# Thirty-two pairs of projections of an fp32 transformer layer turned from eight half products each into seven

## The chip, the cores and the metric

One core of a Trainium2 chip runs the whole program in one launch. The metric is the device time of that core in microseconds, the median over the runs. Each comparison with the kernel before is made on the same chip.

## The reference, cut to what matters

The program computes two blocks in fp32. The second block normalises 512 tokens of 2048 features (`h`) and projects them by one wide matrix `w_in_2` into pooling, sliding-window attention (SWA), gated linear attention (GLA), memory attention and four merge gates:

```
p = h @ w_in                      # h: 512 x 2048
pool_v, pool_g, swa q/k/v (12 heads x 128), swa gate (4 x 128), gla ..., mem q, mem gate (4 x 128), gates
y_pool = pool_mixer(v, g)         # running means over 2, 4, 8, 16 tokens minus the input, a 256 x 256 mix, silu(gate)
y_swa  = for 4 heads: 3 dilated windows (dilation 1, 4, 16), merged by their log-sum-exp, silu(gate)
y_mem  = softmax(q k^T) v over 256 memory tokens, silu(gate)
z_b    = y_b @ w_br_b             # one per branch
merged = sum_b sigmoid(gate_b) * z_b
out    = rms_norm(... + merged @ w_out)
```

SWA, memory and pooling together read 64 blocks of 128 columns of `w_in_2`: 40, 8 and 16 of them.

## The kernel before

A fp32 product is made as three passes of a rounded format: the high part of an operand is its rounded copy, the low part is what rounding left, and high x high, high x low and low x high are added in PSUM. Activations are kept as `ht_hi` and `ht_lo`. A weight half (1024 rows x 128 columns, 512 KB) lands in one of four slots of `raw`; ScalarE writes its high part into `w_hi`, and GpSimd subtracts (`low_rows`, L756) to get `w_lo`. A unit is one block of 128 output features for all 512 tokens: two halves, 16 slices of 128 rows, 48 matmuls of 512 columns (`accumulate`, L785), in one of the PSUM banks `proj0`, `proj1`.

The order of every engine is written out by hand; semaphores join the engines. From 1451 us on the second block runs so: SWA (4 heads x 10 units, the attention of a head stands inside the units that follow), memory (4 heads x 2 units), `zs` (the SWA output by its branch matrix), pooling (4 groups x 4 units), `zm`, `zp`. Then comes the merge gate stage of 32 pairs: two blocks of 128 columns at once, split in two also along the 2048 rows and along the tokens, made by a Strassen-Winograd scheme of seven half products instead of eight. One half product (`product`, L1556) is 8 matmuls of 512 columns (weight high part by [high | low] of 256 tokens) and 8 of 256 columns (weight low part by high). The scheme needs sums of activation quarters (`s1_f` and so on, L3568 to L3588), made once while `zp` runs, and for each pair differences of weight quarters (`t_w`, `raw` minus `raw`) and sums of results out of PSUM. In this stage VectorE makes all seven low parts (L3593) and the four differences, and GpSimd is idle.

Of the kernel before, what the change touches and what calls it, by code (L numbers as in the profile page):

```python
# [12 lines left out]
P = 128  # L13
# [35 lines left out]
          ("xq", 8, 4), ("xwo", 8, 16), ("gv", 16, 2), ("gla", 32, 16), ("zg", 16, 14), ("swa", 80, 40),  # L49
          ("mem", 16, 8), ("zs", 8, 16), ("pool", 32, 16), ("zm", 8, 16), ("zp", 16, 16), ("wout2", 32, 16)]  # L50
# [41 lines left out]
EARLIER = 16  # L92


class Events:
# [34 lines left out]
def build(nc, a, out, stop=None):  # L130

    with ExitStack() as ctx:
# [50 lines left out]

        dist = keep("dist", [P, T])
# [14 lines left out]
        lru_half_c, lru_hba, lru_hbx = small[:, 20:24], small[:, 24:28], small[:, 28:32]  # L199

# [142 lines left out]
        po = Region((m_at + 32768, m_end), (kv1_at, kv1_at + 8192), (kv2_at, kv2_at + 8192))  # L343
        p_w = at("p_w", [P, 4, 2, 2, P], kv1_at)
        po.stretches.pop(1)
        p_u = [po(f"p_u{i}", [P, 16 + T]) for i in range(2)]
        s_at = [po.stretches[0][0] + 2112 * i for i in range(2)]
        p_s = [po(f"p_s{i}", [P, 16 + T]) for i in range(2)]
        p_ph = [at(f"p_ph{i}", [P, T], s_at[i] + 64, F32R) for i in range(2)]
        p_z, p_rc = po("p_z", [P, T]), po("p_rc", [P, 4, 16])  # L350
        po.stretches.pop(0)
        p_at = po.stretches[0][0]
        p_p = [po(f"p_p{i}", [P, T]) for i in range(2)]
        p_pl = [at(f"p_pl{i}", [P, T], p_at + 2048 * i, F32R) for i in range(2)]
        p_wh, p_wl = po("p_wh", [P, 2, 2, P], F32R), po("p_wl", [P, 2, 2, P], F32R)
        mm = Region((m_at + 32768, m_end), (kv1_at, kv1_at + 8192))
        c_q, c_z0, c_z1 = [mm(f"c_{n}", [P, T]) for n in "q z0 z1".split()]
        c_z = [c_z0, c_z1]
        c_st = mm("c_st", [P, 12])
        c_l = at("c_l", [P, 1024], kv1_at)  # L360
        c_pt = at("c_pt", [P, 2, T], kv1_at + 4096)
# [3 lines left out]
        x3t = at("x3t", [P, NT, D], m_at)  # L365
        g_row = at("g_row", [P, D], m_at + 32768)
        y_tok = at("y_tok", [P, NT, D], xy_at)
# [8 lines left out]
        YH_XA, YH_GLA, YH_SWA, YH_MEM, YH_POOL, YH_END = 0, 4, 12, 16, 20, 28  # L376
# [10 lines left out]
        def need(eng, s, n):  # L387
# [39 lines left out]
        swa_act = events("swa_act", "e2 w z n0 n1 n2 n3 c0 c1 c2 c3")  # L427
# [8 lines left out]
        pool_pe, pool_act, pool_dve = events("pool_pe", "mix"), events("pool_act", "z0 hi0 z1 hi1"), \  # L436
            events("pool_dve", "p y0 y1")
        pool_wh, pool_ph, pool_lo = [sem(f"pool_{n}") for n in "wh ph lo".split()]
        ml_gate, ml_conv, ml_var = events("ml_gate", "rows"), sem("ml_conv"), sem("ml_var")
# [79 lines left out]
        def _(sp):  # L519
# [118 lines left out]
            def swa_loads(b, i):  # L638
                for g in range(SWA_GROUPS):
                    for u, c in enumerate((C_SV, C_SQ, C_SK)):  # L640
                        unit(b, 6 * g + 2 * u, w2, i * P + c + g * SWA_HPG * P)
                unit(b, 18, w2, i * P + C_SG)
            loop("swa", SWA_HPG, 20, swa_loads)

            def mem_loads(b, i):
                unit(b, 0, w2, i * P + C_MQ)
                unit(b, 2, w2, i * P + C_MG)
            loop("mem", MEM_HEADS, 4, mem_loads)

# [29 lines left out]
            def gate_loads(m, b, first, last):  # L679
# [46 lines left out]
        def _(pool):  # L726
# [34 lines left out]
            with pool.Fori(1, H4["wout2"]) as i:  # L761
                low_rows(i)
# [6 lines left out]
        def _(pe):  # L769
# [294 lines left out]
            def probs_t(n, l, geo, ts):  # L1064

                offs = [sum(g[1] for g in geo[:t]) * P for t in range(NT)]
                for t in ts:
                    pe.wait_ge(att_w, n * 4 + t + 1)
                    if t >= 2:
                        pe.wait_ge(att_c, n * 4 + t - 1)  # L1070
                    transposes(TB[t % 2], [l[:, offs[t] + x * P:offs[t] + (x + 1) * P] for x in range(geo[t][1])]
                               ).then_inc(att_p, 1)
# [325 lines left out]
            def swa_scores(qb, i, g):  # L1398

                taken(qb, 3 * g + 1)  # L1400
                if g:
                    wait(pe, swa_dve, "l03", i)
                else:
                    pe.wait_ge(yh_f, i + XA_HEADS)
                k0 = i * 9 + 3 * (MO_HEADS + g)
                for t in range(NT):
                    if t < NT - 1:
                        pe.wait_ge(att_k, k0 + t + 1)
                    else:
                        taken(qb, 3 * g + 2)  # L1410
# [7 lines left out]
                if g:  # L1418
                    ins.then_inc(swa_pe.sem, 1)

# [34 lines left out]
            def swa_behind(i):  # L1455

                def step(x):
                    if x:
                        swa_values(i, x - 1)
                    swa_probs(i, x)  # L1460

                return {1: lambda: swa_back(i), **{8 + 2 * x: (lambda x=x: step(x)) for x in range(4)}}

            def swa_head(b, qb, i, before):

                for g in range(SWA_GROUPS + 1):
                    if g == 0:
                        unit(b, 0, qb, 0, behind=swa_behind(i - 1) if before else {})
                    else:
                        then = {1: lambda: swa_scores(qb, i, g - 1)}  # L1470
                        if g == SWA_GROUPS:
                            then[9] = lambda: swa_natural(i)
                        unit(b, 6 * g, qb, 3 * g, behind=then)
                    if g == SWA_GROUPS:
                        break
                    unit(b, 6 * g + 2, qb, 3 * g + 1, behind={2: lambda: swa_values(i - 1, 3)} if before and g == 0 else {})
                    taken(qb, 3 * g)
                    v_t((yh_f, i + XA_HEADS), w_v)
                    unit(b, 6 * g + 4, qb, 3 * g + 2)

            swa_head(H4["swa"], Q2["swa"], 0, False)
            with pe.Fori(1, SWA_HPG) as i:
                swa_head(i * 5 + H4["swa"], i * 5 + Q2["swa"], i, True)


            def mem_probs(i):

                def step(ts):
                    pe.wait_ge(yh_f, i + 8)
                    probs_t(i + A_MEM, c_l, FULL, ts)  # L1490

                return {11: lambda: step((0, 1)), 14: lambda: step((2, 3))}

            def mem_values(i):

                values(i + A_MEM, c_pt, lambda blk: v2[:, i, blk, :], FULL)

            for i in range(MEM_HEADS):
# [2264 lines left out]
```

## Time and profile before

| | us |
|---|---|
| median of 3 runs | 3201.99 (3201.89 to 3205.3) |
| span of the profiled execution | 3201.1 |
| TensorE busy | 3186.8 (100%) |
| VectorE busy | 1341.0 (42%) |
| ScalarE busy | 1290.4 (40%) |
| GpSimd busy | 1063.6 (33%) |

The profiled execution gives only its span of 3201.1 us; its own time is not shown, and it can't be further from the runs than the 0.9 us between that span and their median plus what lies around the span. "Busy" of TensorE includes matmuls whose ends are modelled, so stage lengths are read from starts.

### The profile page before, as it was taken

What the parts mean: (1) busy time and instruction counts of PE and PEld (TensorE: products, weight loads), DVE (VectorE), ACT (ScalarE), POOL (GpSimd) and SP (SyncE); (2) the same over time, 40 slices, a digit from 0 to 9 for tenths busy, and PEclk for the clock granted to TensorE, in tenths of its full rate; (3) what the DMA queues carried; (4) which work ended last, traced back from release to release, by engine and by line L of the source; (5) the groups of instructions that cost most, each with busy time, mean ns of one, the idle gap of its engine ahead of it and who ended that gap; (6) DMA issues with size and microseconds to landing.
All of it is one profiled execution on the core that took longest, in us unless ns stands there. A gap on an engine that the chain in (4) does not pass through costs nothing.

```text
span 3201.1 us, 41942 instructions
## 1 busy us (share of the span) xinstructions
PE 3186.8 (100%) x15426; PEld 2665.0 (83%) x15426; DVE 1341.0 (42%) x1885; ACT 1290.4 (40%) x1992; POOL 1063.6 (33%) x460
## 2 busy tenths in 40 slices
PE   9999999999999999999999999999999999999999
PEld 8877888888888888888888888888888888888887
DVE  3573321113123534401111111144369999999802
ACT  6543322333235534332323324422335555555532
POOL 7633333333443434443433433344430000000043
PEclk9999999999999999999999999999999999999999
DMA  8622323233433423243333333433444444444442
GB/s 291 179 79 67 86 66 86 79 85 98 120 107 100 144 74 93 80 134 102 86 86 92 87 84 92 133 104 92 150 133 134 140 137 138 134 134 134 143 153 99
DMA packets 546540, 364.49 MB, mean 114 GB/s; under 512 B 18809, under 2 KB 505209, under 8 KB 545145
## 3 DMA queue, kind: packets, MB, share of 16 engines
q1 hardware_dynamic: 522912, 321.50, 35.3%
q10 hardware_dynamic: 23512, 41.40, 3.7%
q8 instruction: 79, 1.29, 0.2%
q14 instruction: 37, 0.30, 0.0%
HBM read 333.49 MB, written 29.36 MB: 113 GB/s over the span
## 4 chain that ended last, share of the span: by engine, by line
PE 97%; DVE 1%; ACT 1%; POOL 0%; issue 0%; DMA 0%; DVEq 0%; ACTq 0%; POOLq 0%
PE proj L785 59%; PE s L1556 10%; PE t L1556 8%; PE s L1600 3%; PE proj L1556 1%; PE s L1255 1%; PE proj L1600 1%; PE t L1600 1%; PE t L810 1%; PE s L854 1%; PE s L847 1%; PE t L1255 1%; PE proj L1255 1%; PE s L1080 1%; PE s L1061 1%; PE s L948 1%
## 5 line engine op out<-in xcount | busy, mean ns | idle before, releaser
L756 POOL TENSOR_TENSOR w_lo<-raw,w_hi 128x1024 fp32r<-128x1024 f32 x431 | 1061.5, 2477 | 2111.6 <-ACT w_hi L1637 2084.7
L785 PE MATMUL proj<-ht_hi,w_hi 128*128 128x512 f32 x2400 | 956.0, 398 | 0.0
L785 PE MATMUL proj<-ht_hi,w_lo 128*128 128x512 f32 x2400 | 935.6, 390 | 0.0
L785 PE MATMUL proj<-ht_lo,w_hi 128*128 128x512 f32 x2400 | 934.8, 389 | 0.0
L1637 ACT ACTIVATE w_hi<-raw 128x1024 fp32r<-128x1024 f32 x396 | 404.3, 1053 | 386.3 <-PE proj L785 223.9
L785 PEld LDWEIGHTS proj<-ht_lo,w_hi 128*128 128x128 f32 x2400 | 451.2, 188 | 95.1 <-issue 4.8
L785 PEld LDWEIGHTS proj<-ht_hi,w_lo 128*128 128x128 f32 x2400 | 450.6, 188 | 95.8
L785 PEld LDWEIGHTS proj<-ht_hi,w_hi 128*128 128x128 f32 x2400 | 451.0, 188 | 94.7 <-issue 4.8
L3593 DVE TENSOR_TENSOR w_lo<-raw,w_hi 128x1024 fp32r<-128x1024 f32 x128 | 156.1, 1219 | 16.0 <-ACT w_hi L2507 14.9
L2511 ACT ACTIVATE w_hi<-t_w 128x1024 fp32r<-128x1024 f32 x96 | 101.9, 1061 | 106.1 <-DVE t_w L3611 53.3
L3593 DVE TENSOR_TENSOR w_lo<-t_w,w_hi 128x1024 fp32r<-128x1024 f32 x96 | 116.9, 1217 | 12.8 <-ACT w_hi L2511 12.8
L2507 ACT ACTIVATE w_hi<-raw 128x1024 fp32r<-128x1024 f32 x96 | 101.7, 1059 | 37.5 <-PE s L1556 18.9
L3395 DVE COPY w_k<-proj 128x128 f32<-128x128 f32 x32 | 7.1, 283 | 245.6 <-PE proj L785 245.6
L785 PE MATMUL proj<-yh,w_hi 128*128 128x512 f32 x240 | 94.5, 394 | 0.0
L785 PE MATMUL proj<-yh,w_lo 128*128 128x512 f32 x240 | 93.4, 389 | 0.0
L785 PE MATMUL proj<-yl,w_hi 128*128 128x512 f32 x240 | 93.4, 389 | 0.0
L3034 DVE COPY a_k<-proj 128x128 f32<-128x128 f32 x24 | 5.3, 284 | 187.7 <-PE proj L785 187.7
L2338 ACT ACTIVATE w_l<-w_l,w_st 128x128 f32<-128x128 f32 (+1 forms) x48 | 20.2, 422 | 134.8 <-DVE w_st L3408 92.4
L1556 PE MATMUL t<-ht_lo,w_hi 128*128 128x512 f32 x256 | 64.1, 392 | 0.0
L1556 PE MATMUL s<-ht_hi,w_hi 128*128 128x512 f32 x256 | 63.7, 391 | 0.0
L1556 PE MATMUL s<-ht_lo,w_hi 128*128 128x512 f32 x256 | 63.5, 390 | 0.0
L3097 DVE TENSOR_TENSOR xy<-proj,n_x 128x512 f32 (+1 forms) x16 | 11.0, 690 | 115.2 <-PE proj L785 110.8
(693 smaller groups left out, 4948.7 us busy)
## 6 DMA issues: line engine op xcount, KB each, us to landing
raw<-in_w_in_dram SPq DMA_DIRECT2D x404, 512.0 KB, 3.8
raw<-in_w_out_dram SPq DMA_DIRECT2D x64, 512.0 KB, 3.9
g_zt<-z_spill SPq DMA_DIRECT2D x64, 256.0 KB, 3.9
raw<-in_xa_wkv_dram SPq DMA_DIRECT2D x16, 512.0 KB, 7.2
raw<-in_w_mem_kv_dram SPq DMA_DIRECT2D x16, 512.0 KB, 3.8
raw<-in_w_br_gla_dram SPq DMA_DIRECT2D x16, 512.0 KB, 4.0
z_spill<-z_early ACTq DMA_DIRECT2D x32, 256.0 KB, 3.1
raw<-in_w_br_pool_dram SPq DMA_DIRECT2D x16, 512.0 KB, 4.2
```

The lines of the kernel that those rows point to most:

```text
L756: pool.tensor_tensor(w_lo[:, slot, :], raw[:, slot, :], w_hi[:, slot, :].bitcast(F32), ALU.subtract).then_inc(lo_done, 1)
L785: ins = pe.matmul(dst, w, x[:, kt, c0:c1], start=first and n == 0 and m == 0, stop=last and n == len(kts) - 1 and m == 2)
L810: ins = pe.transpose(dst[0:m, n * P:n * P + k], src, ident[0:k, 0:k])
L847: pe.matmul(MEM_V[x][blk][:], h[:, kt, c0 + blk * P:c0 + blk * P + P], w, start=kt == 0 and m == 0, stop=kt == KT - 1 and m == 2)
L854: ins = pe.matmul(MEM_K[x][hd // 2][:, hd % 2 * M:hd % 2 * M + M], w, h[:, kt, c0:c0 + M], start=kt == 0 and hd % 2 == 0 and m == 0, stop= ...
L1255: ins = pe.matmul(VB[blk][t][:], x[:, kt, t * P:(t + 1) * P], w, start=kt == 0 and m == 0, stop=kt == KT - 1 and m == 2)
L1556: ins = pe.matmul(dst, w[:, slot, k * P:(k + 1) * P], x[:, k, 0:cols], start=fresh and n == 0 and k == 0, stop=n == 1 and k == 7, skip_gro ...
L1600: ins = pe.matmul(BANKS[fb % 2][t][:], x[:, k, t * P:(t + 1) * P], w, start=k == 0 and m == 0, stop=k == KT - 1 and m == 2)
L1637: act.activation(w_hi[:, slot, :], raw[:, slot, :], ACT.Copy).then_inc(hi_done, 1)
L2507: return act.activation(w_hi[:, (PRODUCTS * b + j) % RING, :], src, ACT.Copy)
L2511: return act.activation(w_hi[:, (PRODUCTS * b + j) % RING, :], t_w[:], ACT.Copy)
L3593: return dve.tensor_tensor(w_lo[:, slot, :], src, w_hi[:, slot, :].bitcast(F32), SUB)
```

## The change

The 64 units of SWA, memory and pooling become 32 pairs of seven half products ("duos"), all ahead of `zs`, `zm` and `zp`, which now follow one another. The activation sums are made while `zg` (the GLA branch product) runs. For every duo ScalarE makes seven high parts, VectorE the low parts of products 0, 1 and 2 (counted from 0), the four weight differences and the sums out of PSUM, and GpSimd the low parts of products 3 to 6. The attention and pooling work of VectorE stands at fixed places of a duo ("front", "window", "middle", "end"), that of TensorE and ScalarE behind numbered steps. Outputs of the heads go to `y_spill` in DRAM and come back for `zs`, `zm`, `zp`; the keys and values of the memory go to DRAM after the first block's LRU part and come back for their stage. Many tiles move in SBUF.

```diff
+            for t in range(DUOS):                                   # GpSimd
+                duo_low(t, 3, "hb22", right(t)[1], "lb22")
+                duo_low(t, 4, "ht3", right(t)[0], "lt3")
+                duo_low(t, 5, "hb21", B21, "lb21")
+                duo_low(t, 6, "ht4", t_w[:], "lt4")
...
+            def duo_pair(t, behind={}):                             # TensorE
+                after(pe, "lb11", t)
+                after(pe, "f21", t - 2)
+                run(0, A, A11, True)
+                after(pe, "lt1", t)
+                after(pe, "c11", t - 1)
+                run(1, TB[1], S1, True)
+                after(pe, "lt2", t)
+                after(pe, "s1", t)
+                run(2, A, S2, False)
+                after(pe, "lb22", t)
+                after(pe, "s5", t)
+                run(3, TB[1], S4, False)
+                after(pe, "lt3", t)
+                after(pe, "v", t)
+                run(4, A, S3, False)
+                after(pe, "lb21", t)
+                after(pe, "f12", t)
+                run(5, TB[1], A12, True)
+                after(pe, "lt4", t)
+                after(pe, "c22", t)
+                run(6, A, A22, False)
...
+            def swa_first(i):                                       # TensorE, steps behind half products
+                return {5: lambda: swa_natural(i), 9: lambda: swa_back(i), 10: lambda: swa_probs(i, 0), 12: second}
...
+            def duo_first(t):                                       # VectorE
+                after(dve, "lt4", t - 1)
+                dve.wait_ge(block_in[0], 16 * t + 32)
+                dve.wait_ge(right_in(t)[0], 16 * t + 32)
+                dve.tensor_tensor(t_w[:], right(t)[0], B11, SUB).then_inc(duo_dve.sem, duo_dve.to("t1", t))
+                duo_low(t, 0, "hb11", B11, "lb11")
+            def duo_second(t):
+                duo_low(t, 1, "ht1", t_w[:], "lt1")
+                ...
+                dve.tensor_tensor(t_w[:], right(t)[1], t_w[:], SUB).then_inc(duo_dve.sem, duo_dve.to("t2", t))
+            def duo_pair(t, before, early, late, behind={}):        # VectorE
+                duo_low(t, 2, "ht2", t_w[:], "lt2")
+                dve.tensor_tensor(right(t)[0], right(t)[1], right(t)[0], SUB).then_inc(duo_dve.sem, duo_dve.to("t3", t))
+                if t:
+                    duo_f21(t - 1, *before)
+                then("front")
+                dve.wait_ge(block_in[3], 16 * t + 32)
+                after(dve, "lt2", t)
+                dve.tensor_tensor(t_w[:], B21, t_w[:], SUB).then_inc(duo_dve.sem, duo_dve.to("t4", t))
+                then("window")
+                after(dve, "sv", t)
+                added(t, d_v[:], rest(A), early_scale, d_v[:], "v")
+                after_product(dve, t, 3)
+                ... c12, f12
+                then("middle")
+                if t < DUOS - 1:
+                    duo_first(t + 1)
+                after_product(dve, t, 4)
+                ... c22, f22
+                if t < DUOS - 1:
+                    duo_second(t + 1)
+                after_product(dve, t, 5)
+                ... c11, f11
+                then("end")
...
+            def swa_first(i):                                       # VectorE
+                def window():
+                    swa_spread(i)
+                    swa_gate(i)
+                    swa_shares(i)
+                return {"window": window, "middle": lambda: swa_classes(i)}
...
+                duo_pair(t, (GATE, 1.0), (NEAR_Q, HEAD_SCALE, scored(i - 1, "s2")), (NEAR_V, 1.0, turned_v(3 * i)),
+                         swa_first(i - 1) if i else {"window": strips})
...
+                    first = {"front": lambda: pool_gate(g - 1, 0), "window": gated_and_mixed}
+                    if g == 2:
+                        first = {**first, "middle": lambda: y_lows(Y_SWA, 0)}
+                    second = {"window": lambda: pool_sums(g), "end": lambda: pool_lows(g)}
...
+            for n in range(KT):                                     # ScalarE, while zg runs
+                branch_z(n // 4, n % 4)
+                if n in (3, 4, 5, 7):
+                    sums_high((3, 4, 5, 7).index(n))
```

`hX` is a high part made by ScalarE, `lX` its low part, `t1` to `t4` weight differences of 128 x 1024, `v`, `c..` and `f..` sums of results (256 or 512 columns), `al`, `s1`, `s5`, `sv` ScalarE's copies out of PSUM.

## Rows read from the trace of the kernel before

**Rows 1.** The merge gate stage by window: us, busy of PE, PEld, DVE, ACT, POOL, clock, DMA.
```profile
2396.00:3020.00 624.00, 624.00 (x3587) 549.86 (x3586) 580.58 (x712) 335.91 (x452) 0.00 (x0) 1.00 0.48 135
```
**Rows 2.** Chain that ended last: start us, us, what.
```profile
1451.52 21.76 PE proj L785 x96
...
2396.42 19.50 PE s L1556 x112
...
3020.02 43.52 PE s L1600 x192
```
**Rows 3.** The same chain, attention and mixing matmuls inside it.
```profile
1604.89 1.52 PE s L1416 x8
...
1695.83 0.44 PE t L810 x4
...
2158.15 2.79 PE s L1532 x12
```
**Rows 4.** VectorE, GLA's end and activation sums: start us, us, engine line op.
```profile
1374.12 1.35 DVE L3287 TENSOR_TENSOR yl<-y_f,yh 128x512 fp32r<-128x512 f32 x2
...
2306.93 2.29 DVE L3568 TENSOR_TENSOR s_f<-ht_hi,ht_lo 128x2048 f32<-128x2048 f32 x1 [40.19 <-PE proj L785]
2309.26 4.36 DVE L3569 TENSOR_TENSOR s_f<-s_f,ht_hi 128x2048 f32<-128x2048 f32 x1
...
2348.56 3.30 DVE L3583 CAST ht_hi<-ht_lo 128x2048 fp32r<-128x2048 f32 x1
```
**Rows 5.** GpSimd in the same stretch.
```profile
2302.64 2.40 POOL L756 TENSOR_TENSOR w_lo<-raw,w_hi 128x1024 fp32r<-128x1024 f32 x1 [3.04 <-ACT w_hi L1637]
2308.08 3.39 POOL L756 TENSOR_TENSOR w_lo<-raw,w_hi 128x1024 fp32r<-128x1024 f32 x1 [3.04 <-ACT w_hi L1637]
```
**Rows 6.** VectorE in the merge gate stage.
```profile
2646.54 1.22 DVE L3593 TENSOR_TENSOR w_lo<-t_w,w_hi 128x1024 fp32r<-128x1024 f32 x1
...
2648.93 0.68 DVE L3617 TENSOR_TENSOR sn<-s,sn 128x512 f32<-128x512 f32 x1
2649.65 0.43 DVE L3619 TENSOR_TENSOR s<-sn 128x256 f32<-128x256 f32 x1
```
**Rows 7.** ScalarE in the merge gate stage.
```profile
2649.12 1.06 ACT L2511 ACTIVATE w_hi<-t_w 128x1024 fp32r<-128x1024 f32 x1 [1.68 <-DVE t_w L3611]
2650.09 0.36 ACT L2586 ACTIVATE dist<-s 128x256 f32<-128x256 f32 x1
```
**Rows 8.** VectorE at SWA's start and in the shares of a head.
```profile
1452.61 0.29 DVE L3359 TENSOR_SCALAR w_strip<-dist 128x256 f32<-128x256 f32 x1 [77.14 <-ACTq L1649]
...
1463.24 0.18 DVE L3387 TENSOR_REDUCE w_st<-w_sel 128x4 f32<-128x16 f32 x1
...
1680.18 0.23 DVE L3426 TENSOR_TENSOR w_sel<-s,w_st 128x64 f32<-128x64 f32 x1 [2.12 <-PE s L1424]
...
1681.27 2.33 DVE L3432 TENSOR_TENSOR w_st<-w_st 128x4 f32<-128x4 f32 x1
...
1685.18 0.19 DVE L3444 TENSOR_TENSOR w_spread<-w_st 128x32 f32<-128x32 f32 x1
```
**Rows 9.** VectorE in memory and pooling.
```profile
1952.64 1.42 DVE L3028 TENSOR_REDUCE c_st<-s 128x1 f32<-128x256 f32 x4 [0.16 <-DVE c_z L3502]
...
2182.01 0.69 DVE L3530 TENSOR_TENSOR p_s<-p_u 128x512 f32<-128x512 f32 x1 [7.89 <-ACT p_u L2475]
```
**Rows 10.** GpSimd beside the first row of Rows 9.
```profile
1952.71 4.77 POOL L756 TENSOR_TENSOR w_lo<-raw,w_hi 128x1024 fp32r<-128x1024 f32 x2 [2.50 <-ACT w_hi L1637]
```
**Rows 11.** ScalarE in `zg`.
```profile
1413.57 0.60 ACT L2280 ACTIVATE z_early<-proj 128x512 f32<-128x512 f32 x1 [3.26 <-PE proj L785]
```
**Rows 12.** Windows of 1 us at the last matmul and behind it.
```profile
3194.00:3195.00 1.00, 0.13 (x1) 0.00 (x0) 0.05 (x1) 0.69 (x2) 0.00 (x0) 1.00 0.96 401
...
3197.00:3198.00 1.00, 0.00 (x0) 0.00 (x0) 1.00 (x3) 0.00 (x0) 0.00 (x0) 0.50 0.49 186
```
**Rows 13.** The chain at the kernel's start.
```profile
2.96 4.53 PE s L869 x20
```

More of the change, by code:

```diff
@@ L350, in build @@
[L350 to L358, printed above, removed]
@@ L435, in build, with after, after_product, w_slot @@
         st_dve = events("st_dve", "c11 f11 f21 lt2 t3 lb22 n2 n2a lt3 t4 lb21 n1 n1a lt4 t1 lb11 c12 c22 f12 f22 lt1 t2")
-        pool_pe, pool_act, pool_dve = events("pool_pe", "mix"), events("pool_act", "z0 hi0 z1 hi1"), \
-            events("pool_dve", "p y0 y1")
+        pool_pe, pool_act, pool_dve = events("pool_pe", "mix"), events("pool_act", "z0 z1"), \
+            events("pool_dve", "p g0 g1 y0 y1")
         pool_wh, pool_ph, pool_lo = [sem(f"pool_{n}") for n in "wh ph lo".split()]
+        pool_w_in, y_out, y_out2 = Again(weights_in, 80), Again(spilled, 64), [Again(x, 128) for x in tile_in]
+        kv2_out, k2_in, v2_in = Again(mlg_in, 16), Again(lr_in, 16), Again(gf_in, 16)
+        y_in = Again(mem_first, 16), Again(par_in, 32), Again(x3_out, 64)
+        y_tile_in = [Again(x, 16) for x in mem_in[1]]
+        y_highs_done, y_ready, zp_apart = Again(mem_hi, 16), Again(mem_ready[0], 16), Again(r_rows, 2)
+        duo_pe = Again(xt_pe, 16)
+        duo_dve = Order(sem("duo_dve"), "lt2 t3 f21 t4 v c12 f12 t1 lb11 c22 f22 lt1 t2 c11 f11", "t1 lb11 lt1 t2", "f21")
+        duo_act = Order(sem("duo_act"), "al hb22 s1 ht3 s5 hb21 sv ht4 hb11 ht1 ht2", "hb11 ht1 ht2", "al")
+        duo_pool = Order(sem("duo_pool"), "lb22 lt3 lb21 lt4")
+        duo = {n: order for order in (duo_dve, duo_act, duo_pool) for n in order.names}
+        def after(eng, name, t):
+            if t >= 0:
+                eng.wait_ge(duo[name].sem, duo[name].value(name, t))
+        def after_product(eng, t, j):
+            eng.wait_ge(duo_pe.sem, duo_pe.done + PRODUCTS * t + j + 1)
+        def w_slot(t, j):
+            return (PRODUCTS * t + j) % RING
         ml_gate, ml_conv, ml_var = events("ml_gate", "rows"), sem("ml_conv"), sem("ml_var")
@@ new lines, in zs_rest @@
+            def zs_rest():
+                for j in range(RING, 8):
+                    pairs(H4["zs"], j, a["w_br_swa_2"][0], j * 2 * P)
+            zs_rest()
+            for y in y_out2:
+                sp.wait_ge(y.sem, y.done + 16 * POOL_GROUPS)
+            y_load(1, Y_MEM)
+            for j in range(RING):
+                pairs(H4["zm"], j, a["w_br_mem_2"][0], j * 2 * P)
+            sp.wait_ge(half_done, th(H4["zs"], 7))
+            y_load(0, Y_POOL)
+            for j in range(RING, 8):
+                pairs(H4["zm"], j, a["w_br_mem_2"][0], j * 2 * P)
@@ L1396, in _, with product @@
             accumulate(b + 3, 3, TB[1][:], range(8), 0, yh, yl, (0, T), True, True)
-            def swa_scores(qb, i, g):
-                taken(qb, 3 * g + 1)
-                if g:
+            A11, A12, S3, A22 = [x[:, k0:k0 + 8, :] for x in (ht_hi, ht_lo) for k0 in (0, 8)]
+            S1, S2, S4 = [x[:].rearrange("p k x n -> p k (x n)") for x in (s1, s2, s4)]
+            def product(g, bank, x, fresh, done, mid=None):
+                slot = g % RING
+                wide = ((w_hi, bank[:], 2 * M), (w_lo, left(bank), M))
+                for n, (w, dst, cols) in enumerate(reversed(wide) if g % 2 else wide):
+                    for k in range(8):
+                        ins = pe.matmul(dst, w[:, slot, k * P:(k + 1) * P], x[:, k, 0:cols], start=fresh and n == 0 and k == 0,
+                                        stop=n == 1 and k == 7, skip_group_check=True)
+                    if n == 0 and mid is not None:
+                        mid()
+                ins.then_inc(done, 1)
@@ new lines, in duo_pair, with run @@
+            def duo_pair(t, behind={}):
+                g, A = PRODUCTS * t, proj[t % 2]
+                def run(j, bank, x, fresh):
+                    product(g + j, bank, x, fresh, duo_pe.sem, behind[2 * j + 1] if 2 * j + 1 in behind else None)
+                    if 2 * j + 2 in behind:
+                        behind[2 * j + 2]()
+                after(pe, "lb11", t)
[19 more added lines that the diff above has]
+                run(6, A, A22, False)
@@ L1419, in swa_scores, with swa_vt @@
                     ins.then_inc(swa_pe.sem, 1)
+            def swa_vt(i, g):
+                after(pe, "f21", SWA_DUOS * i + (0, 1, 3)[g])
+                if g == 0 and i:
+                    wait(pe, swa_act, "c3", i - 1)
+                elif g:
+                    pe.wait_ge(att_vc, i * 3 + MO_HEADS + g)
+                transposes(TB[0], blocks(w_v)).then_inc(att_vt, 1)
             def swa_natural(i):
@@ L1460, in step @@
                     swa_probs(i, x)
[L1462 to L1479, printed above, removed]
@@ L1498, in _ @@
[L1498 to L1507 removed]
+                return {2: lambda: step(2), 4: lambda: step(3), 6: lambda: swa_values(i, 3), **other}
@@ new lines, in _, with mem_scores @@
+            pe.wait_ge(sums_ready, 4)
+            bank_wait(Q2["zs"], 0)
+            pe.wait_ge(z_apart, 2)
+            for i in range(SWA_HPG):
+                swa_head(i)
+            def mem_scores(i):
+                after(pe, "f21", MEM_DUO + i)
+                if i == 0:
+                    pe.wait_ge(k2_in.sem, k2_in.done + 16)
+                    wait(pe, swa_act, "c3", SWA_HPG - 1)
+                    pe.wait_ge(yh_f, XA_HEADS + SWA_HPG)
+                scores(i + A_MEM, c_q, k2b[:, i, :], FULL)
@@ new lines, in _ @@
+            pe.wait_ge(y_ready.sem, y_ready.done + Y_POOL + 4)
+            for u, bank in enumerate(opened):
+                if u < 2:
+                    bank_wait(qb, u)
+                accumulate(b, u, bank[:], range(4), 0, y_hi[0], y_lo[0], (0, T), True, False, part=True)
+            for u, bank in enumerate(opened):
+                accumulate(b, u, bank[:], range(4), 4, y_hi[1], y_lo[1], (0, T), False, True,
+                           fresh=(y_ready.sem, y_ready.done + Y_POOL + 4) if u == 0 else None)
@@ new lines, in _ @@
+            duo_pair(MEM_DUO + 1, (MEM_Q, HEAD_SCALE), (MEM_G, 1.0, nothing), (MEM_Q, HEAD_SCALE, mem_free(1)),
+                     {"front": lambda: mem_gate(0), "window": lambda: swa_y(last), "end": lambda: mem_logits(0)})
+            for i in range(2, MEM_HEADS):
+                duo_pair(MEM_DUO + i, (MEM_Q, HEAD_SCALE), (MEM_G, 1.0, nothing), (MEM_Q, HEAD_SCALE, mem_free(i)),
+                         {"front": lambda: mem_gate(i - 1), "window": lambda: mem_inverted(i - 2),
+                          "middle": lambda: mem_y(i - 2), "end": lambda: mem_logits(i - 1)})
```

1087 lines of the change are left out of this document (664 added, 423 removed).

## The prediction

> **What bounds the kernel now.** I read the chain that ended last first. From 1451 to 3020 us it is TensorE nearly throughout, and two paces stand in it: 96 matmuls of units take 21.76 us, so a unit of 48 takes 10.88 and two units 21.76; the 32 pairs of the merge gate stage take 3020.02 - 2396.42 = 623.60 us, 19.49 each and 2.784 per half product [rows 2]. Attention and mixing matmuls stand between them (1.52 us of scores, 0.44 of transposes, 2.79 of a pooling mix) [rows 3]. TensorE is thus the bound, and less work for it is worth its full time, if the others keep pace. The window of the gate stage says how near they are: VectorE is busy 580.58 us of 624, 18.1 per pair, with GpSimd at nothing [rows 1]. The change mixes these two worlds: half products, but with GpSimd at work. So I looked last for what the two engines do to each other.
>
> **VectorE beside GpSimd.** A subtraction of 2048 elements out of SBUF takes VectorE 2.29 us; the next, just alike in size, takes 4.36 [rows 4]. It started at 2309.26 while GpSimd was at a low part from 2308.08, which itself took 3.39 where one alone takes 2.40 [rows 5]: GpSimd waited until VectorE's first operation ended at 2309.22, ended at 2311.47, and only then VectorE ran. So they take turns, whole operations at a time, and one that waits comes next; a GpSimd low part holds VectorE for about 2.25 us. A tiny operation of 4 elements also pays it: 2.33 [rows 8]. Four maxima over PSUM take 1.42 us in all [rows 9] in the midst of GpSimd's 4.77 us [rows 10], so work with one input in PSUM does not pay. The Trainium skill (SBUF — State Buffer, "Who interferes with whom") puts it as a lock: two SBUF inputs on VectorE against a GpSimd operation that reads SBUF, held for the whole instruction. It adds that issue order decides who blocks; were VectorE always first, its chain would lose nothing and only GpSimd's slack would go, which is the first rival's case.
>
> **The gain.** 32 x (21.76 - 19.49) = 72.8 us [rows 2]. Attention, mixing and branch matmuls stay as many.
>
> **A duo without other work.** Time counts from the start of half product 0; product j would start at 2.784 j. Durations: low part or difference of 1024 elements 1.22 (1.14 from start to start), 512 elements 0.68, 256 0.43 [rows 6]; high part 1.06, `al` 0.36 [rows 7]; GpSimd 2.4. VectorE runs from the end of `lt4` on GpSimd: t1 and lb11 of the next pair, c22 (2.3 to 3.0 after it), f22, lt1, t2 (from 4.6), then c11 and f11, but lt2 only after ScalarE's ht2 at 7.0; lt2 to 8.2, t3 to 9.3. GpSimd has asked for lb22 by then and holds until 11.6; t4 waits for it and ends at 12.8; then lt3, lb21, lt4 end at 15.1, 17.5 and 19.9. The loop closes in 20.0 us: as long as TensorE's 19.49 within my error, and no slack for either. Added up, both engines' work on shared inputs is 8.0 + 0.8 + 4 x 2.3 = 18 us of it. TensorE's attention work, where there is some, is hidden room for this loop, so an empty duo costs 0 to 0.5 us; I take 0 and price what is put into it.
>
> **Where it stalls.** t4 ends some 5.9 us into a duo, product 4 would start at 11.1 and waits for `v`, which VectorE issues only after "window". Behind it, in order, stand c12, f12, "middle", t1, lb11, c22, for which products 5, 0 (next) and 6 wait.
> - `strips`, first duo: 10.8 us from 1452.61 to 1463.42, of which 3.9 is waiting [rows 8]; 6.9 plus up to four low parts (9.2) from 2.2 us on ends at 18.3: 7.6 late. Below: with no low part between, 9.1, nothing. Before it TensorE waits 0.8 for ScalarE's copy of the last `zg` bank.
> - A head's shares (4 times): spread waits behind lt3 until 8.2, and TensorE, behind product 2's middle, for spread (1 us); the gate behind lb21 until 11.3; then the chain from 1680.18 to 1685.37 less 2.6 of waiting [rows 8] with lt4 between its first operations. It ends at 15.9, v at 16.3: 5.2 late each, 20.8. Below: without waits 9.5, nothing; above 8 each.
> - The classes, `y`, logits of 3.1 and 1.5 us read PSUM and fit into the 4.8 us free in the window or the head's room: 0.
> - Memory, duos 21 to 24: maxima of 1.42 us at "end" [rows 9] push lt2, t3, ht3, and ScalarE's weighting waits for an inverse behind t4, so the transposes behind it come 2 to 3 us late: 1, 2.5, 2.5 and 3.5 (with the pads), 9.5; 0 to 16.
> - Pooling, second duo of each group: 2 x (g + 2) operations of 0.73 and four small ones of 0.2 per group g, two SBUF inputs each [rows 9]: s = 3.7, 5.1, 6.6, 8.0 us. None of it can run beside lt3, lb21, lt4 (6.9). v comes at about 6.1 + 6.9 + s + 0.6, so 2.5 + s late: 6.2 (7 with a memory head), 7.6, 9.1, 10.6. The first duo has 2.79 us of mixing on TensorE [rows 3] as room and costs nothing, but for g = 2 (four low parts of y in "middle"), 1.5. Sum 35.8; if half of the low parts met nothing, 16; with every loop spilling over, 45.
> - `zg`: the sums start at 1375.5, when GLA's last low part is done, and the fourth needs 44.9 us [rows 4], to 1420.4; ScalarE stands at `sums_high` until then and 1.9 us more, and has copied bank 8, ready at 1413.57 [rows 11], only at 1423; unit 10 wants it at 1419.0. With smaller ones before it 5 us; 0 if GpSimd, starved by ScalarE, blocks less.
>
> Sum: 8.4 + 20.8 + 9.5 + 35.8 + 5 = 79.5 us. Late starts of `zs`, `zm`, `zp` I put at nothing: the reloads of y have over 10 us of branch units each as cover; if that fails, some 3 us each. The spills and the 2 MB of keys and values go out beside unit work.
>
> **The clock.** A gap has a second price. The granted clock is 1.00 while TensorE works, and 0.50 in the window 3197 to 3198, three us after the last matmul [rows 12]. At the start 20 transposes took 4.53 us, 0.227 each, against 0.11 in the middle of the kernel [rows 3, 13]: the lower of the two levels, kept for some 5 us, which costs 2.5 us of work. Five gaps here are above 6 us (2.5 each) and four near 4 (half of that, since the row puts the fall just there): 17.5 us; from 0 to 25. In a sentence apart: the Trainium skill (TensorE: Matmul & The Clock Gate, "What's actually happening") says the same of a pause and of the way back, and by it the four near 4 us would count in full, 22.5.
>
> 3201.1 - 72.8 + 79.5 + 17.5 = 3225.3 in the profiled execution; with the 0.9 us between its span and the median, 3226.
>
> **Rivals.**
> 1. *The turns seldom collide* (0.30). GpSimd's low parts fall where VectorE waits for TensorE, or VectorE is first. For it: the gate stage ran 18.1 us of VectorE per pair without a stall, and GpSimd's deadlines are 4 us off. Against: in the sums of rows 4 half of the operations paid. Stalls of 25 us, no clock loss: 3202 - 73 + 25 = 3154. Up to 72.8 of stalls it stays faster: this is the other side.
> 2. *The clock holds through the gaps* (0.20): 3209. For it: each gap is followed and preceded by dense work; against, rows 12. 0.08 of it, with fewer stalls, is within 0.2%.
> 3. *The loop of 20.0 is 1 us longer everywhere* (0.10): handovers add, and every duo without attention on TensorE stalls as well, ScalarE's waits too: 3226 + 30 = 3256.
> 4. *The forecast* (0.40): gain eaten by VectorE and GpSimd taking turns, clock loss on top.
>
> 0.2% (6.4 us) is about what can be told from no change here. Faster: rival 1, 0.30. Same: 0.08. Slower: 0.12 + 0.10 + 0.40 = 0.62. The range leaves out the better half of rival 1 and the far end of 3: 3160 to 3256. The forecast's own, by its bounds, is 3205 to 3250.
>
> **What would show it.** Right: in the gate stage nothing changes (19.49 per pair); a GpSimd low part in SWA to pooling means above 2.6 us, VectorE's small operations in the shares show some of 2.3; product 4 waits for `v` on VectorE in duos 0, 5, 10, 15, 20 and, growing by 1.5 us, in 25, 27, 29, 31; windows around them show a clock below 1.00; the empty duos 3, 8, 13 take 20.4. The 32 duos with their attention take 79.5 - 5 + 17.5 = 92 us more than 32 x 19.49 and the old attention work. Wrong: pooling duos near 19.5 us would mean that the turns cost little and the time is near 3150; a stall before product 6 in every duo means rival 3; long stalls named by DMA would mean that I missed the weights, whose slots are here freed by GpSimd's late low parts.

## The result and the profile after

The changed kernel took 3218.27 us (median of 4 runs, 3216.48 to 3221.14) beside 3202.56 for the kernel before (4 runs, 3201.89 to 3205.3): a ratio of 1.005, 95% interval 1.0036 to 1.0064: slower by half a percent, clear of noise. The forecast was 3226, slower. The profiled execution took 3221.14 us with a span of 3219.1 and a mean granted clock of 0.989.

In the page of the changed kernel the busy line of each engine reads (busy us, share of the span, instructions):

```profile
PE 3135.8 (97%) x15938; PEld 2650.3 (82%) x15938; DVE 1780.5 (55%) x2330; ACT 1422.6 (44%) x2180; POOL 1099.8 (34%) x460
```

TensorE fell from 100% to 97% of the span: it has less to do and waits more. The span grew by 18.0 us (3219.1 - 3201.1), and all of that stands before the merge gate stage. Its chain, that answers to [rows 2]:

```profile
2414.80 19.45 PE s L1559 x112
...
3037.73 43.52 PE s L1829 x192
```

The stage starts 18.38 us later (2414.80 against 2396.42) and lasts 622.93 us where it lasted 623.60. So 72.8 + 18.4 = 91.2 us were lost on the way to it, where 72.8 is the gain that the forecast counted on. The windows of the duos show where, SWA first, then memory, then pooling (us, busy of PE, PEld, DVE, ACT, POOL, clock, DMA share, GB/s):

```profile
1456.00:1920.00 464.00, 445.46 (x2601) 391.54 (x2602) 351.35 (x451) 231.06 (x397) 221.11 (x84) 0.98 0.35 98
1920.00:2050.00 130.00, 122.87 (x681) 104.31 (x679) 94.16 (x118) 68.67 (x136) 51.92 (x21) 0.97 0.32 90
2050.00:2232.00 182.00, 148.32 (x772) 126.26 (x772) 148.95 (x167) 69.70 (x94) 76.23 (x29) 0.91 0.35 101
```

TensorE lacks 18.5, 7.1 and 33.7 us in them. Every wait of TensorE of 0.4 us or more from 1360 to 2420, added up, is 68.2 us; the kernel before has none there. The rest is the clock. I took windows of 0.5 us over the same stretch and summed TensorE's busy time times (1 - clock) in each: 23.1 us of work, in 11 places, of 1.6 to 3.2 us. 68.2 + 23.1 = 91.3, against 91.2 by the starts of the stage.

The last pooling group is the longest gap, 2207.76 to 2217.90. The chain there (start us, us, what):

```profile
2200.15 3.00 DVE t_w L3783
2203.16 2.82 DVE p_s L4022
2205.99 2.77 DVE p_s L4022
2208.79 2.72 DVE p_s L4022
2211.53 0.70 DVE p_s L4022
...
2216.31 0.70 DVE p_p L4025
2217.90 5.15 PE proj L1559 x16
```

and GpSimd beside it (idle time before and its releaser in brackets):

```profile
2198.72 9.49 POOL L905 TENSOR_TENSOR w_lo<-raw,w_hi 128x1024 fp32r<-128x1024 f32 x3 [8.37 <-ACT w_hi L2550]
2208.17 2.79 POOL L905 TENSOR_TENSOR w_lo<-t_w,w_hi 128x1024 fp32r<-128x1024 f32 x1
```

The same addition on VectorE takes 2.8 us while GpSimd's four low parts run, from 2198.72 to 2210.96, and 0.70 once they are done. t4 (L3783) pays 1.8 us and three additions 2.0 to 2.1 each: 8.0 us, ahead of `v`, for which the product waits. The clock behind this gap, and behind those of groups 2 and 1:

```profile
2217.90:2222.00 4.10, 4.10 (x14) 3.62 (x15) 0.81 (x2) 2.17 (x4) 2.38 (x1) 0.50 0.02 4
2164.00:2168.00 4.00, 4.00 (x14) 3.53 (x15) 3.08 (x4) 2.17 (x4) 0.00 (x0) 0.51 0.02 4
2108.80:2113.00 4.20, 4.20 (x14) 3.72 (x15) 3.00 (x4) 2.09 (x4) 0.00 (x0) 0.50 0.02 6
```

TensorE is busy through all three at half its clock (14 matmuls in 4.1 us).

### The profile page after: what moved, and what is told of

The parts are those of the page before. It is cut to its first block, busy times and chain, and to the rows that moved or that the text cites. A ratio compares the mean times of both kernels' runs of the same rounds, so it can differ in the third digit from the quotient of the medians.

```text
span 3219.1 us, 43126 instructions
## 1 busy us (share of the span) xinstructions
PE 3135.8 (97%) x15938; PEld 2650.3 (82%) x15938; DVE 1780.5 (55%) x2330; ACT 1422.6 (44%) x2180; POOL 1099.8 (34%) x460
## 4 chain that ended last, share of the span: by engine, by line
PE 84%; DVE 10%; POOL 2%; issue 2%; ACT 1%; DMA 1%; DVEq 0%; ACTq 0%; SPq 0%; POOLq 0%
PE proj L937 35%; PE t L1559 13%; PE s L1559 10%; PE proj L1559 7%; PE s L1829 3%; POOL w_lo L905 2%; DVE w_lo L3734 2%; PE proj L1829 1%; PE s L1407 1%; PE t L1829 1%; DVE p_s L4022 1%; PE t L962 1%; PE s L962 1%; PE s L1006 1%; PE s L999 1%
## 5 line engine op out<-in xcount | busy, mean ns | idle before, releaser
L937 PE MATMUL proj<-ht_hi,w_hi 128*128 128x512 f32 x1376 | 549.2, 399 | 0.0
L937 PE MATMUL proj<-ht_hi,w_lo 128*128 128x512 f32 x1376 | 536.6, 390 | 0.0
L937 PE MATMUL proj<-ht_lo,w_hi 128*128 128x512 f32 x1376 | 535.9, 389 | 0.0
L905 POOL TENSOR_TENSOR w_lo<-raw,w_hi 128x1024 fp32r<-128x1024 f32 x96 | 262.4, 2748 | 411.7 <-ACT w_hi L2550 411.7
L937 PEld LDWEIGHTS proj<-ht_lo,w_hi 128*128 128x128 f32 x1376 | 258.6, 188 | 56.0 <-issue 3.8
L937 PEld LDWEIGHTS proj<-ht_hi,w_hi 128*128 128x128 f32 x1376 | 258.5, 188 | 55.4 <-issue 3.8
L937 PEld LDWEIGHTS proj<-ht_hi,w_lo 128*128 128x128 f32 x1376 | 258.3, 188 | 54.7
L2550 ACT ACTIVATE w_hi<-t_w 128x1024 fp32r<-128x1024 f32 x96 | 101.6, 1059 | 174.8 <-DVE t_w L3741 90.2
L2550 ACT ACTIVATE w_hi<-raw 128x1024 fp32r<-128x1024 f32 x128 | 135.0, 1055 | 34.5 <-PE t L1559 20.8
L2852 ACT ACTIVATE w_hi<-t_w 128x1024 fp32r<-128x1024 f32 x96 | 102.0, 1062 | 105.4 <-DVE t_w L4137 52.6
L1559 PE MATMUL proj<-ht_lo,w_hi 128*128 128x512 f32 x512 | 135.1, 408 | 11.5 <-DVE d_v L3757 7.8
L1559 PEld LDWEIGHTS proj<-ht_lo,w_hi 128*128 128x128 f32 x512 | 97.9, 197 | 34.1 <-issue 14.7
L1559 PE MATMUL proj<-ht_lo,w_lo 128*128 128x256 f32 x512 | 76.8, 295 | 30.2 <-DVE d_v L3755 30.2
L937 PE MATMUL proj<-y_hi,w_hi 128*128 128x512 f32 x240 | 94.2, 393 | 6.8 <-ACT z_late L2511 4.5
L1559 PE MATMUL t<-s4x,w_hi 128*128 128x512 f32 x384 | 100.4, 405 | 0.0
```

Source lines behind the costliest of these rows:

```text
L905: pool.tensor_tensor(w_lo[:, w_slot(t, j), :], src, w_hi[:, w_slot(t, j), :].bitcast(F32), ALU.subtract).then_inc(duo_pool.sem, duo_pool.t ...
L937: ins = pe.matmul(dst, w, x[:, kt, c0:c1], start=first and n == 0 and m == 0, stop=last and n == len(kts) - 1 and m == 2)
L1559: ins = pe.matmul(dst, w[:, slot, k * P:(k + 1) * P], x[:, k, 0:cols], start=fresh and n == 0 and k == 0, stop=n == 1 and k == 7, skip_gro ...
L2550: act.activation(w_hi[:, w_slot(t, j), :], src, ACT.Copy).then_inc(duo_act.sem, duo_act.to(name, t))
L2852: return act.activation(w_hi[:, (PRODUCTS * b + j) % RING, :], t_w[:], ACT.Copy)
```

## The experiments

The theory was the forecast's: gaps because VectorE and GpSimd take turns where two SBUF inputs meet a low part (L905 on GpSimd), and lost clock on top. Rivals: the gaps are VectorE's own load, whoever makes the low parts; or the loop of copies, differences and sums is too long in itself. Each kernel is a variant of the changed one. "Gaps" is the sum of TensorE's waits of 0.4 us or more, "lost clock" the sum described above.

**All seven low parts on VectorE.**

```diff
-  duo_dve = "lt2 t3 f21 t4 v c12 ..."
-  duo_pool = "lb22 lt3 lb21 lt4"
+  duo_dve = "lt2 t3 f21 lb22 t4 lt3 lb21 v lt4 c12 ..."
+  duo_pool = ""
```

> VectorE makes all seven low parts of a duo, GpSimd none; nothing else changes. Theory (the two engines take turns on operations with two SBUF inputs, and the turns hold product 4 back): VectorE's own work grows by 4 x 1.14 us per duo, but no operation of it waits for GpSimd. Shares end near 12 us, v some 1 us late; the pooling duos wait for v by s - 2.3 us, 1 to 6, where they now wait 3.9 to 10.1; gaps of the 32 duos 25 instead of 61 us, time about 3165. Rival A (VectorE is short of time whoever makes the low parts, and GpSimd relieves it): 4.6 us more per duo on VectorE, time 3218 plus 30 to 80. Rival B (latency from product to product is the cause): no change beyond 5 us.

Measured: 3169.98 us (3164.91 to 3171.12), ratio to before 0.9894 [0.9878, 0.9911], 5 us above the expected 3165. Gaps 29.7, lost clock 8.4. 128 more operations on VectorE made the kernel 48 us faster, so the first rival is out. VectorE's busy time rose by only 29.6 us (1780.5 to 1810.1), though 128 low parts of 1.14 from start to start are 146: by this difference some 116 us of its busy time in the changed kernel were waiting, since the profile counts an operation that waits for its turn as busy. The same additions in the last pooling group of this kernel:

```profile
2157.36 0.68 DVE L4021 TENSOR_TENSOR p_s<-p_u 128x512 f32<-128x512 f32 x1
2158.08 2.14 DVE L4021 TENSOR_TENSOR p_s<-p_s 128x512 f32<-128x512 f32 x3
```

four in 2.86 us, against 9.1 in the changed kernel. Its gap is 4.74 us instead of 10.14.

**Two low parts of four on GpSimd, and one.** GpSimd keeps lb22 and lb21, then lb21 alone; VectorE has the others in the places of the first experiment.

```diff
-  duo_pool = "lb22 lt3 lb21 lt4"
+  duo_pool = "lb22 lb21"        # the second kernel: "lb21"
```

> GpSimd keeps the low parts of products 3 and 5 (lb22, lb21), VectorE makes the other five. Theory: what costs is each turn of GpSimd (2.25 us of VectorE's waiting against 1.14 us for VectorE's own work), so the time stands between none (3170) and four (3218): 3180 to 3195. Rival A (GpSimd relieves a short VectorE, and four are only too many): two are better than none, under 3170.

> GpSimd keeps one low part per duo, that of product 5 (lb21), at whose time VectorE would often wait for product 3 anyway. Theory: within 5 us of none, 3165 to 3178; the pooling duos, where VectorE is short, lose 1 us each. Rival A: 3160 or less.

Measured: 3187.9 us (3186.52 to 3191.93), ratio 0.9959 [0.9944, 0.9973], gaps 43.9, lost clock 15.2; and 3181.14 (3176.16 to 3184.85), ratio 0.9929 [0.9912, 0.9945], gaps 36.2, lost clock 18.2. The first falls as expected. The second is a miss, 3 us outside. With none, one, two and four low parts on GpSimd the time is 3170, 3181, 3188 and 3218. One low part per duo lengthens the gaps by 6.4 us only (36.2 - 29.7, unrounded); the other 9.8 in the profiled executions is the clock (18.2 - 8.4). Gaps of 1.97, 1.88 and 0.83 us with nothing behind them in the first kernel are 2.33, 3.30 and 1.92 here, and a stretch of half clock follows each. In the last pooling group one addition of three meets the one low part, on VectorE and on GpSimd:

```profile
2169.27 0.68 DVE L4022 TENSOR_TENSOR p_s<-p_u 128x512 f32<-128x512 f32 x1
2169.99 4.23 DVE L4022 TENSOR_TENSOR p_s<-p_s 128x512 f32<-128x512 f32 x3
```

```profile
2169.81 2.41 POOL L905 TENSOR_TENSOR w_lo<-raw,w_hi 128x1024 fp32r<-128x1024 f32 x1 [18.76 <-ACT w_hi L2547]
```

4.23 - 2.14 = 2.09 us.

**The pooling sums behind `v` instead of ahead of it.**

```diff
   added(t, d_v[:], ..., "v")
+  then("behind v")
...
-  second = {"window": lambda: pool_sums(g), "end": ...}
+  second = {"behind v": lambda: pool_sums(g), "end": ...}
```

> The pooling sums stand behind v instead of ahead of it in the second duo of each group; same operations on every engine. Theory: product 4 then starts on time and product 5 waits for f12, s us late where product 4 was 2.5 + s late; 2.5 us less per group and shorter gaps: 3205 to 3210. Rival A (VectorE's total work is the bound): the gap only moves, 3218. If the turns with GpSimd weren't the reason, the sums would find 4 us free behind v and the gaps would shrink to s - 4, some 20 us less in all: 3198.

Measured: 3207.55 us (3204.13 to 3210.08), ratio 1.0014 [1.0005, 1.0024]; gaps 59.9, lost clock 17.5. As expected. The product that waits for `v` goes through and the next one waits, for f12, behind the same sums: the gaps of the three later groups are 5.4, 6.8 and 7.8 instead of 7.4, 8.8 and 10.1. The place of the sums decides a quarter of these gaps, not more.

**The pooling additions with one input in PSUM.** The doubling additions read a score bank as their second input, so the sums hold other values.

```diff
-  link(dve.tensor_tensor(dst[...], src[...], src[:, 16 - d:16 - d + T], ADD))
+  link(dve.tensor_tensor(dst[...], src[...], S[2 + x][:], ADD))
```

> In the pooling sums the second input of each of the 20 doubling adds is read from a PSUM bank instead of SBUF (the pooled values are thus other ones); same number, size and order of operations. Theory: such an add doesn't take turns with GpSimd. The window then runs beside lt3, lb21 and lt4; the three gaps of groups 1 to 3 (7.4, 8.8, 10.1 us) shrink by 4 to 6 us each, the time by 15 to 20 us to about 3200. Rival A or B: the same operations take VectorE the same time, so nothing changes, 3218.

Measured: 3208.83 us (3204.03 to 3212.2), ratio 1.0015 [1.0005, 1.0025]; gaps 58.2, lost clock 22.3. Less than expected: 9 us instead of 15 to 20. VectorE in the last group shows both the mechanism and why the size was off:

```profile
2193.28 3.08 DVE L3783 TENSOR_TENSOR t_w<-raw,t_w 128x1024 f32<-128x1024 f32 x1
2196.29 0.68 DVE L4022 TENSOR_TENSOR p_s<-p_u,s 128x512 f32<-128x512 f32 x1
2197.00 2.13 DVE L4022 TENSOR_TENSOR p_s<-p_s,s 128x512 f32<-128x512 f32 x3
2199.17 2.38 DVE L4025 SCALAR_TENSOR_TENSOR p_p<-p_s,p_u 128x512 f32<-128x512 f32 x1
2201.58 2.19 DVE L4027 TENSOR_TENSOR p_p<-p_s,p_rc 128x16 f32<-128x16 f32 x1
```

With an input in PSUM the four additions take 2.8 us, as if GpSimd were not there. The wait went to whatever has two SBUF inputs next: a row of 512 that takes 0.69 now takes 2.38, one of 16 elements 2.19 instead of 0.17. Three operations now wait (t4, 3.08, and these two) where four did: one turn was saved, and the gaps fell to 6.0, 6.7 and 7.2. The Trainium skill (SBUF — State Buffer, "Who interferes with whom") says that an operation of VectorE with at most one SBUF input, outside its two-port modes, does not contend with GpSimd; these rows agree.

**The three long gaps filled for the clock.** Idle transposes ahead of the wait for `v` keep TensorE at work.

```diff
+FILL = {27: 50, 29: 60, 31: 72}
...
   after(pe, "lt3", t)
+  for _ in range(FILL.get(t, 0)):
+      pe.transpose(S[3][:, 0:P], ident[:], ident[:])
   after(pe, "v", t)
```

> 50, 60 and 72 idle transposes (0.11 us each at the higher clock) are run by TensorE in the gaps ahead of product 4 of duos 27, 29 and 31, whose length they don't exceed. Theory (a gap has a second price, the lower clock behind it): the granted clock stays 1.00 there and the three gaps cost 1.5 to 2.5 us less each: 3212 to 3214. Rival (the time behind a gap is VectorE's anyway, or the clock isn't TensorE's limit there): 3218.

Measured: 3210.9 us (3206.34 to 3212.99), ratio 1.0023 [1.0012, 1.0034]. The kernel does 182 matmuls more and is 7.4 us faster by the medians (3218.27 - 3210.9), a little more than expected; gaps 46.4, lost clock 16.9 instead of 23.1. The fill left 1.9 to 2.2 us of each gap open. Behind two of them the clock still fell, for less long; behind the last it did not:

```profile
2106.00:2111.00 5.00, 5.00 (x20) 4.12 (x20) 3.46 (x6) 2.59 (x4) 0.00 (x0) 0.66 0.18 43
2160.50:2166.00 5.50, 5.50 (x22) 4.56 (x22) 3.97 (x6) 3.11 (x5) 0.00 (x0) 0.69 0.24 61
...
2214.00:2220.00 6.00, 6.00 (x36) 5.35 (x37) 2.28 (x5) 4.11 (x7) 4.25 (x2) 1.00 0.10 31
```

The three places together lose 3.4 us of work where they lost 6.6: the fill gave back 3.2 us, less than the 4.5 to 7.5 that was expected of it. Another 3.0 us of the fall in lost clock stand behind gaps that the edit leaves alone, and 2.0 come from a wait in the later branches (2.06 instead of 4.06). Each kernel has one trace, so these two may be chance, and so may be the match of the time with what was expected.

So the experiment shows the clock's price as apart from the wait, but smaller than the 7.4 us say. That the clock does not hold (rival 2) is shown by the changed kernel itself, in the three windows at 0.50.

**The first experiment, with the extra work split.** All low parts on VectorE; the strips go half into the first and half into the second duo; each pooling sum goes half ahead of `v`, half behind it.

```diff
-  second = {"window": lambda: pool_sums(g), ...}
+  second = {"window": lambda: pool_sums(g, 0), "behind v": lambda: pool_sums(g, 1), ...}
...
-  {"window": lambda: swa_y(i - 1)} if i else {}
+  {"window": (lambda: swa_y(i - 1)) if i else strips_rest}
```

> All seven low parts on VectorE; the strips are split over the windows of duos 0 and 1, and of each group's pooling sums one half stands ahead of v and the other behind it. Theory: the gap of 4.1 us in duo 0 goes, those of 1.9, 4.3 and 4.7 in the pooling duos shrink to 1 to 3, since product 4 and then product 5 each wait for half of the work; 5 to 8 us less than with all on VectorE alone: 3162 to 3165. If VectorE's total is the bound there, the pooling gaps only move: 3166.

Measured: 3161.68 us (3157.52 to 3165.08), ratio 0.9871 [0.9855, 0.9888], the fastest of all, 40 us under the kernel before in the same comparison (3201.98), and at the fast end of what was expected. Gaps 25.7, lost clock 6.8. The busy line of its page, and the window of its duos:

```profile
PE 3120.2 (99%) x15938; PEld 2637.8 (83%) x15938; DVE 1815.1 (57%) x2458; ACT 1422.4 (45%) x2180; POOL 760.2 (24%) x332
1456.00:2171.00 715.00, 699.40 (x4052) 608.77 (x4052) 627.31 (x862) 368.75 (x625) 9.02 (x4) 1.00 0.38 106
```

TensorE is back at 99%. VectorE, the engine that seemed in want of help, is at 57% of the span and at 88% in the duos (627.31 of 715), and the duos still hold. By the median it is 8.3 us under the first experiment, though the two kernels ran apart and the intervals of their ratios overlap a little ([0.9878, 0.9911] and [0.9855, 0.9888]); the first gap, duo 0's, went from 4.09 to 1.38, and the longest in the last two groups from 4.26 and 4.74 to 2.10 and 2.82.

**The account.** For each kernel 3201.1 - 72.8 + gaps + lost clock should be its span:

| low parts on GpSimd | gaps | lost clock | by the account | span |
|---|---|---|---|---|
| 4 (the change) | 68.2 | 23.1 | 3219.6 | 3219.1 |
| 4, sums behind `v` | 59.9 | 17.5 | 3205.7 | 3205.3 |
| 4, PSUM input | 58.2 | 22.3 | 3208.8 | 3209.8 |
| 2 | 43.9 | 15.2 | 3187.4 | 3185.8 |
| 1 | 36.2 | 18.2 | 3182.7 | 3182.9 |
| 0 | 29.7 | 8.4 | 3166.4 | 3166.9 |
| 0, work split | 25.7 | 6.8 | 3160.8 | 3160.8 |

It closes to 1.6 us or better in all seven. The kernel with the filled gaps stands apart, since its 182 transposes are work that the others don't have: at 0.11 us each they are 20.0, and 3128.3 + 46.4 + 16.9 + 20.0 = 3211.6, against 3211.2. No loss much above 1.6 us is left over, and the gain of 72.8 is right.

## Why the prediction was right, and where its terms were not

The direction and the mechanism held: the gain is eaten where VectorE and GpSimd take turns, with the clock on top. The terms summed to 79.5 + 17.5 = 97.0; the trace has 68.2 + 23.1 = 91.3. That is nearer than the terms are, and in part luck: the terms that were too high are so by 18.1 us together, those that were too low by 12.4.

- **The gain, 72.8:** holds by the account, and the gate stage is unchanged.
- **Empty duos, 0:** right. Of the first five duos only duo 1 has nothing for VectorE beside its own work; duos 2 and 3 have logits in their windows and duo 4 at its end, so the "empty duos 3, 8, 13" of the forecast are not quite empty. From 1481 to 1573, which holds duos 1 to 4, TensorE does not stop once:

```profile
1481.00:1573.00 92.00, 92.00 (x539) 81.08 (x539) 70.08 (x82) 46.60 (x77) 45.65 (x17) 1.00 0.33 92
```

  Duo 1 takes 19.93 us from its first matmul to that of duo 2, and duo 3 takes 20.44, as forecast (20.4). The loop of 20.0 us was an upper end; rival 3 has nothing for it.
- **The start, 8.4:** 7.0 (0.89 before the first duo, 6.14 in it). The strips paid four turns, as supposed, one of them before these rows (L3833, 2.40):

```profile
1462.84 2.03 DVE L3835 TENSOR_SCALAR w_l<-dist,w_sel 128x128 f32<-128x128 f32 x1
1464.91 2.32 DVE L3836 TENSOR_SCALAR w_strip<-w_l 128x128 f32<-128x128 f32 x1
1467.27 2.36 DVE L3837 TENSOR_TENSOR w_strip<-w_strip,w_l 128x128 f32<-128x128 f32 x1
1469.66 0.23 DVE L3838 TENSOR_SCALAR w_l<-w_l 128x128 f32<-128x128 f32 x1
```

  The first three of them in the kernel before, where two of the strips' operations paid a turn, this first one and the one that answers to L3833:

```profile
1456.93 2.02 DVE L3369 TENSOR_SCALAR w_l<-dist,w_sel 128x128 f32<-128x128 f32 x1
1458.99 0.23 DVE L3370 TENSOR_SCALAR w_strip<-w_l 128x128 f32<-128x128 f32 x1
1459.25 0.29 DVE L3371 TENSOR_TENSOR w_strip<-w_strip,w_l 128x128 f32<-128x128 f32 x1
```

- **The shares, 20.8:** 11.8 (2.58, 1.63 + 1.66, 2.58, 1.64 + 1.73). This is the mis-sized step: "then the chain ... with lt4 between its first operations". In the first head spread and gate pay a turn, and the small operations behind them run in 2.6 us with none:

```profile
1573.91 2.37 DVE L3875 TENSOR_TENSOR w_spread<-w_st 128x64 f32<-128x64 f32 x1
1576.19 2.87 DVE L3917 SCALAR_TENSOR_TENSOR w_z<-w_z,w_g 128x512 f32<-128x512 f32 x1
1579.10 0.22 DVE L3884 TENSOR_TENSOR w_sel<-s,w_st 128x64 f32<-128x64 f32 x1
...
1581.55 0.19 DVE L3902 TENSOR_TENSOR w_spread<-w_st 128x32 f32<-128x32 f32 x1
```

  lt4 is not there yet: GpSimd idles 3.40 us before it, because ScalarE makes ht4 only behind the exponential of the shares (L2659), which itself waits for VectorE.

```profile
1573.70 4.82 POOL L905 TENSOR_TENSOR w_lo<-raw,w_hi 128x1024 fp32r<-128x1024 f32 x2 [2.26 <-ACT w_hi L2550]
1581.91 2.41 POOL L905 TENSOR_TENSOR w_lo<-t_w,w_hi 128x1024 fp32r<-128x1024 f32 x1 [3.40 <-ACT w_hi L2550]
```

```profile
1580.41 0.21 ACT L2659 ACTIVATE w_st<-w_st 128x12 f32<-128x12 f32 x1 [4.85 <-DVE w_st L3892]
1580.53 0.36 ACT L2605 ACTIVATE d_v<-proj 128x256 f32<-128x256 f32 x1
1580.79 1.05 ACT L2550 ACTIVATE w_hi<-t_w 128x1024 fp32r<-128x1024 f32 x1
```

  The chain starves its own disturber. It is so in all four heads: GpSimd idles 3.40 to 3.47 us before lt4. A turn of 2.3 us less per head takes the 20.8 to 11.6. I had placed lt4 by TensorE's pace and not walked ScalarE's order of work. And 1 us was put on TensorE's wait for spread, which cost up to 2.58; where it cost that, in two heads, product 4 did not wait for `v` at all.
- **Memory, 9.5:** 6.4 (1.47, 1.92, 1.86, 1.18), ScalarE's weighting late, as named.
- **Pooling, 35.8:** 33.7. The second duos have 3.85, 7.38, 8.82 and 10.14 against 7, 7.6, 9.1 and 10.6; 1.47 and 2.02 elsewhere against 1.5. From group 1 on they grow by about the 1.5 us a group that the sum of VectorE's own additions gives, and the price of the low parts ahead of them is right. Why group 0 has 3.85 and not 7 stays open.
- **`zg`, 5:** 2.5, by the mechanism named but one sum earlier. The copy that TensorE waited for, at 1409.65, stands behind ScalarE's high part of the third sum (1407.84), which waited 8.64 us for VectorE. Behind the fourth sum, where the forecast had the 5 us, the copy came at 1421.92, as late as forecast, and TensorE did not stop.
- **The later branches, 0:** 6.8, a miss. TensorE waits 2.30 before `zs`' second unit for VectorE's last result and 4.06 further on for ScalarE's copy of a bank (and 0.46 for another such copy):

```profile
2288.89 1.06 ACT L1866 ACTIVATE w_hi<-raw 128x1024 fp32r<-128x1024 f32 x1 [7.27 <-DMA raw<-in_w_br_mem_dram]
2289.85 0.58 ACT L2511 ACTIVATE z_late<-proj 128x512 f32<-128x512 f32 x1
```

  The copy stands behind a high part that waits for a weight transfer, and SyncE issues that one right behind a reload of y, for which it had waited 18.5 us on a unit of TensorE:

```profile
2278.30 0.37 SPq L727 DMA_DIRECT2D y_raw<-y_spill  x1
2278.71 3.61 SPq L686 DMA_DIRECT2D raw<-in_w_br_mem_dram  x4
```

  That "the reloads of y have over 10 us of branch units each as cover" was said of the reloads' own data and left out what stands behind them in SyncE's queue. The wait stays, at 3.8 to 3.9 us, with all low parts on VectorE too, so it does not hang on GpSimd's low parts. No experiment changed the order of that queue.
- **The clock, 17.5:** 23.1. The size per place was right for the long gaps (2.3, 2.0 and 2.3 behind 7.38, 8.82 and 10.14; I had 2.5). The failing step was the count, "above 6 us (2.5 each) and four near 4 (half of that", with smaller gaps at nothing: five of the eleven places, 9.9 us of the 23.1, are behind gaps of 1.86 to 2.58.

## What to carry to other kernels

Before an elementwise operation goes to GpSimd to relieve VectorE, count what it holds up and not only what it takes off: here a low part is 1.14 us of VectorE's own work, and one on GpSimd makes it wait up to 2.2, most of all where a chain of small operations stands ahead of something that TensorE waits for. Read an engine's room in the stretch that the change touches, not over the span: here VectorE, busy for 88% of the duos, did all the low parts and the kernel was faster than with GpSimd's help, most so with the work that comes in between split over two places. Price every gap of TensorE as its length plus some 2 us when the clock falls behind it, and walk each engine's queue in its own order, also that of the engine that only issues the transfers.

## What the runs showed of the hardware

- A gap's clock price hardly depends on its length. In the changed kernel 11 places lose 1.6 to 3.2 us of work each, behind gaps from 1.86 to 10.14 us; gaps of 1.47, 1.63, 2.02 and 2.30 have nothing behind them, and neither has one of 2.82 in the last experiment. The fall can come when TensorE is back at work: the gap of 2.58 ends at 1576.33, the next microsecond is still at full clock, and

```profile
1577.00:1581.00 4.00, 4.00 (x13) 3.09 (x12) 3.48 (x10) 0.59 (x3) 1.52 (x1) 0.57 0.80 222
```

  With GpSimd at one low part, the clock was still 1.00 through the first 5.3 us of a gap of 6.20 us (2173.70 to 2179.89) and 0.50 in the five us of dense work behind it:

```profile
2174.00:2179.00 5.00, 0.00 (x0) 0.00 (x0) 4.72 (x9) 0.00 (x0) 0.00 (x0) 1.00 0.22 75
2180.00:2185.00 5.00, 5.00 (x16) 4.32 (x17) 1.64 (x3) 2.06 (x4) 2.38 (x1) 0.50 0.00 0
```

- An operation's size hardly matters for the turn that it waits: 16 elements paid 2.0 us (2.19 against 0.17), 1024 paid 1.9 (3.08 against 1.22), both in the kernel with the PSUM input.
- A TENSOR_SCALAR with one tensor from SBUF waited as well: 2.32 us at 1464.91 with GpSimd at work beside it, 0.23 in the kernel before (L3370), just behind GpSimd's last low part there. The Trainium skill (SBUF — State Buffer, "Who interferes with whom") lists it among those that can take both ports, so one input is no safeguard for this form.
